# Reordering the attention steps of a hybrid backbone kernel, with earlier loads and splits

## What is computed

```python
h = modulate(rms_norm(x, g_mix[l]), mod[:, :, 0], mod[:, :, 1])
p = h @ w_in[l]                      # 6 kinds of features and 3 gates
# 4 retention heads (dk 128, dv 256), 8 latent heads (64+32 by 128),
# 8 grouped-query heads (128) over 2 key/value heads
s = jnp.einsum('bqhgd,bshd->bhgqs', q, k) * scale
pr = jax.nn.softmax(s, axis=-1)
o = jnp.einsum('bhgqs,bshe->bqhge', pr, v)
gs = jax.nn.sigmoid(gates)
z = gs[:, :, 0] * (y_ret @ w_ret_o) + gs[:, :, 1] * (y_mla @ w_mla_o) + gs[:, :, 2] * (y_gqa @ w_gqa_o)
x = x + mod[:, :, 2] * (z @ w_out)
x = x + mod[:, :, 5] * swiglu(modulate(rms_norm(x, g_ffn[l]), mod[:, :, 3], mod[:, :, 4]))
```

## Time and profile before

| | us |
|---|---|
| median of 3 runs | 3534.91 |
| lowest and highest run | 3522.54, 3536.19 |
| the profiled execution | 3530.96 |
| its span | 3528.8 |
| PE busy in it | 3240.0 |
| DVE, ACT, POOL busy | 1519.6, 1254.8, 397.4 |

### The profile page before, as it was taken

The page is one execution under the profiler, slowest core; times in us unless marked ns, Lnnn a source line. Parts: engine busy times, 40 slices in busy tenths (PEclk is TensorE's granted clock), DMA queues, the critical chain, the costliest instruction groups (busy, mean ns, idle before and its releaser), DMA issues.

```text
span 3528.8 us, 49714 instructions
## 1 busy us (share of the span) xinstructions
PE 3240.0 (92%) x18760; PEld 2735.5 (78%) x18760; DVE 1519.6 (43%) x2047; ACT 1254.8 (36%) x1777; POOL 397.4 (11%) x304
## 2 busy tenths in 40 slices
PE   6999999999898889999999978998999898889998
PEld 5788877888777777788888867877777776668886
DVE  4555424445335533422222355553455445443333
ACT  3344432454333332211211234444355433432222
POOL 0011100111101201000100101110011101011001
PEclk9999999999999999999999999999999999999999
DMA  4222141111331143123142432222221232222222
GB/s 181 78 71 73 64 136 63 60 54 59 101 121 64 42 137 126 48 96 112 64 135 70 140 111 81 75 82 84 75 71 65 75 115 68 90 100 95 95 95 101
DMA packets 100921, 315.17 MB, mean 89 GB/s; under 512 B 11088, under 2 KB 21456, under 8 KB 100816
## 3 DMA queue, kind: packets, MB, share of 16 engines
q1 hardware_dynamic: 55872, 202.40, 17.2%
q10 hardware_dynamic: 44944, 111.32, 9.4%
HBM read 283.79 MB, written 29.88 MB: 89 GB/s over the span
## 4 chain that ended last, share of the span: by engine, by line
PE 45%; issue 8%; DVE 5%; ACT 2%; POOL 1%; DMA 1%; ACTq 0%; DVEq 0%; POOLq 0%
PE ps L1417 43%; PE ps L1531 1%; POOL ptl L1399 1%; DVE mx L927 1%; ACT wh L431 1%; PE ps L1509 1%; DVE wl L896 1%; DVE ptl L945 0%; DMA mraw<-in_wmod 0%; DVE tmp L906 0%; DVE tmp L1061 0%; DVE tmp L966 0%; ACT pth L484 0%; PE ps L1441 0%; ACT side L509 0%
## 5 line engine op out<-in xcount | busy, mean ns | idle before, releaser
L1417 PE MATMUL ps<-hh,wh 128*128 128x512 f32 x2768 | 827.2, 359 | 48.5 <-DVE wl L896 25.8
L1417 PE MATMUL ps<-hl,wh 128*128 128x512 f32 x2768 | 818.8, 356 | 0.0
L1417 PE MATMUL ps<-hh,wl 128*128 128x512 f32 x2768 | 815.5, 355 | 0.0
L896 DVE TENSOR_TENSOR wl<-raw,wh 128x1024 fp32r<-128x1024 f32 x364 | 484.1, 1330 | 645.6 <-ACT wh L431 616.1
L1417 PEld LDWEIGHTS ps<-hh,wh 128*128 128x128 f32 x2768 | 454.9, 191 | 138.3 <-issue 48.6
L1417 PEld LDWEIGHTS ps<-hh,wl 128*128 128x128 f32 x2768 | 455.6, 191 | 78.3
L1417 PEld LDWEIGHTS ps<-hl,wh 128*128 128x128 f32 x2768 | 455.0, 191 | 73.8 <-issue 0.7
L431 ACT ACTIVATE wh<-raw 128x1024 fp32r<-128x1024 f32 x364 | 382.5, 1051 | 228.7 <-PE ps L1417 193.2
L1417 PE MATMUL ps<-yh,wh 128*128 128x512 f32 (+1 forms) x1296 | 412.0, 372 | 27.5 <-DVE wl L896 15.1
L1417 PE MATMUL ps<-yl,wh 128*128 128x512 f32 (+1 forms) x1296 | 398.3, 362 | 0.0
L1417 PE MATMUL ps<-yh,wl 128*128 128x512 f32 (+1 forms) x1296 | 397.4, 361 | 0.0
(11 more groups left out here) (190 smaller groups left out, 3452.5 us busy)
## 6 DMA issues: line engine op xcount, KB each, us to landing
raw<-in_stream SPq DMA_DIRECT2D x364, 512.0 KB, 3.5
mraw<-in_wmod ACTq DMA_DIRECT2D x40, 512.0 KB, 3.5
prob<-in_wmod ACTq DMA_DIRECT2D x40, 512.0 KB, 3.5
gspill<-prob ACTq DMA_DIRECT2D x32, 384.0 KB, 2.3
tmp<-gspill ACTq DMA_DIRECT2D x24, 384.0 KB, 3.1
early_y<-in_wmod SPq DMA_DIRECT2D x12, 512.0 KB, 14.6
vraw<-gspill ACTq DMA_DIRECT2D x16, 384.0 KB, 3.5
dec<-in_dec ACTq DMA_DIRECT2D x8, 768.0 KB, 4.2
```

The lines of the kernel that those rows point to most:

```text
L896: dve.tensor_tensor(wl[:, s, :], raw[:, s, :], wh[:, s, :].bitcast(F32), ALU.subtract).then_inc(sem("w_lo"), 1)
L1417: ins = pe.matmul(out, lhs[w], rhs[x](cols), start=start and n == 0, stop=stop and n == 2)
```

## The change

**Attention.** PE's step becomes: scores n, transposes of tile n-2, `fill(n)`, and on odd n a values block of tiles n-3 and n-2. ACT's and DVE's parts on the transposed tile move to the front (ACT) and ahead of `fill` (DVE). `y_hi` and `y_lo` stay behind `fill(n)` on even n. `OUTS` moves to bank 7 and `QSUM` to bank 5, so that scores 1 and 3 wait for `y_lo`, and `LAG` of y falls from 2 to 1. The queries' statistics move by `gqa_stat`: to step 3 in layer 0 and step 1 in layer 1.

```diff
-LAG = {"s_rinv": 1, "s_pn": 1, "t_ready": 2, "t_hi": 2, "t_lo": 2, "y_ready": 2, "y_hi": 2, "y_lo": 2}
+LAG = {"s_rinv": 1, "s_pn": 1, "t_ready": 2, "t_hi": 2, "t_lo": 2, "y_ready": 1, "y_hi": 1, "y_lo": 1}
...
+def gqa_stat(nq):
+
+    return nq - 3
...
-        OUTS = SCORES[0] + TOK
-        QSUM = SCORES[1] + TOK
+        OUTS = SCORES[1] + TOK
+        QSUM = SCORES[0] + TOK
...
-                        if n in (0, 2) and c.has(n - 5):
-                            pe.wait_ge(sem("y_lo"), c.v("y_lo", n // 2 - 3))
-
-                        if n == 3 and std is not None:
+                        if n in (1, 3) and c.has(n - 5):
+                            pe.wait_ge(sem("y_lo"), c.v("y_lo", (n - 5) // 2))
+
+                        if n == 2 and c.nq == 4 and std is not None:
                             pe.wait_ge(sem("v_std"), std)
...
-                    if n == 2:
-
-                        pe.wait_ge(sem("s_exp"), c.v("s_exp", 1))
-                    fill(n)
-                    if n % 2 == 0 and c.has(n - 3):
-                        values(c, n, par if n >= 3 else 1 - par)
                     m = n - 2
...
                         ins.then_inc(sem("t_ready"), 1)
+                    if n == gqa_stat(c.nq):
+                        pe.wait_ge(sem("s_exp"), c.v("s_exp", n - 1))
+                    fill(n)
+                    if n % 2 and c.has(n - 2):
+                        values(c, n, par if n >= 3 else 1 - par)
 
             def values(c, n, vpar):
-                m = n - 3
+                m = n - 2
...
-                    fill(n)
-                    if n % 2 == 0 and c.has(n - 3):
-                        y_lo(c, n // 2 - 2, home)
                     m = n - 2
...
+                    fill(n)
+                    if n % 2 == 0 and c.has(n - 3):
+                        y_lo(c, n // 2 - 2, home)
```

```diff
                     split(at, 7)
+                    split(at, 8)
...
-                    if query and n == 0:
+                    if query and n == 0 and not alone:
                         split(at, c0 + 1)
...
-                            if j == 0:
-                                split(at, 3)
+                            split(at, 2 * j + 3)
```

```diff
+            def first_load(ph):
+
+                if ph["nmod"]:
+                    mod_load(ph, 0, ph["j0"] + ph["home"] * N_MOD * KT)
...
                 elif kind == "z":
+                    first_load(ph["out"])
...
-                            mod_load(ph, 0, row0)
...
                                 if ph["nmod"] and begun:
                                     if k == 1:
-                                        mod_fold(t, r)
-                                    if k != r:
-                                        mod_row(t, k, ph)
+                                        if r:
+                                            mod_fold(t, 0)
+                                        mod_row(t, r, ph)
...
+                        if ph["nmod"] and begun:
+                            mod_fold(t, 1)
```

```diff
-                        pe.wait_ge(sem("v_lo"), t.v("v_lo"))
...
                         split(t, 2)
+                        roped(t, (0, 0), 0, 0, 1, qh, ql, 0, nt)
                         dve.wait_ge(sem("vt_hi"), t.v("vt_hi", 1))
...
-                        roped(t, (0, 0), 0, 0, 1, qh, ql, 0, nt)
```

More of the change, by code:

```diff
@@ L147, in plan @@
         raws = [SPILLED] * MLA_RAWS
-        phase("mla_first", layer, 0, {}, total(head, head, HELD, *raws, attention(nq, first=1)), nt=nt)
+        phase("mla_first", layer, 0, {}, total(
+            head, head, HELD, {"free0": -1, "free1": 1}, *raws, attention(nq, first=1)), nt=nt)
         phase("mla", layer, MLA_HEADS // 2 - 1, total(head, head, att, att, *raws, *raws), nt=nt)
@@ L192, in plan @@
     phase("final", DEPTH - 1, 0, {}, {}, nt=LAT)
-    for ph, after in zip(phases, phases[1:]):
+    for n, (ph, after) in enumerate(zip(phases, phases[1:])):
+        if ph["kind"] in ("z", "ffn"):
+            ph["out"] = next(x for x in phases[n:] if x["kind"] == "out")
         if ph["kind"].endswith("_last"):
@@ L492, in y_hi, with spill @@
                                ACT.Copy).then_inc(sem("y_hi"), 1)
-            def spill(at, kc, f, kg, nt, full, held_at, skip):
-                slot = 1 if held_at is not None and kg == 0 else 0
+            def spill(at, kc, f, kg, nt, full, slot, held_at, skip):
                 act.wait_ge(sem("product"), at.v("chunk", kc + 1))
@@ L551, in fill @@
                 def fill(n):
-                    if query and n == 0:
+                    if query and n == 0 and held_at is None:
                         split(at, c0 + 1)
@@ L991, in fill @@
                     for j, steps in enumerate(pieces):
-                        if n == steps[0]:
+                        if n == steps[0] and not (qslot and j == 0):
                             split(at, c0 + query + j + 1)
@@ L1592, in gqa_query, with raw @@
                 qs, pieces = gqa_steps(nt // P, raws, alone)
+                def raw(n):
+                    for j, steps in enumerate(pieces):
+                        if alone and n == steps[0] and j == 0:
+                            pe.wait_ge(sem("vt_lo"), at.v("vt_lo"))
+                        gate(at, c0 + query + j, j if alone else f0 + query + j, steps, n, nt, 1 - j if alone else 0)
                 def fill(n):
@@ L1602, in fill @@
                         ins.then_inc(sem("v_stat"), 1)
-                    for j, steps in enumerate(pieces):
-                        if alone and n == steps[0] and j == 0:
-                            pe.wait_ge(sem("vt_lo"), at.v("vt_lo"))
-                        gate(at, c0 + query + j, j if alone else f0 + query + j, steps, n, nt, 1 - j if alone else 0)
+                    if not alone or n != 1:
+                        raw(n)
                 return fill
```

65 lines of the change are left out of this document (35 added, 30 removed).

## The result

The changed kernel takes 3620.57 us in the median of four runs (3609.28 to 3628.53). The kernel before took 3530.35 beside it, and the ratio is 1.0255, with a 95% interval of 1.0215 to 1.0295: 2.5% slower, 90 us where 64 were forecast. It lies inside the stated range of 3530 to 3645. Single executions that took far longer than the others of their kernel (3811 and 4195 us of the kernel before, 9062 us of the one with the first heads' part alone) are left out of every ratio here. The profiled execution is 97.6 us longer than that of the kernel before (spans 3626.4 and 3528.8).

What follows compares the result with a forecast made beforehand. TensorE, busy 92% of the span, was taken as the bound. Waits +84, clock +35 and gains -55 gave +64 on the profiled run's 3530.96, so 3595, or 3599 for the median; range 3530 to 3645.

Steps and rivals of the forecast that it cites:

- Rival B: Whole kernel: the waits come but the clock stays; 3564, nearer 3555 if the chains are shorter; chance 0.25.
- C: Whole kernel: gains fail or are paid back, slow multiplication's 8 added; 3599 + 25 to 45, some 3635; chance 0.10.
- A: Whole kernel, the forecast itself: y stands behind the fill and clock falls follow; 3599; chance 0.45.
- kl waits in retention below 4: Sign in the profile after: PE's waits for kl in retention below 4; if they remain, C.
- Rival D: Scores 1 and 3: ACT and DVE reach y sooner, so PE doesn't wait; near 3468, faster; chance 0.12.
- The clock: Attention heads: long new waits make PE's clock fall, about 24 falls at 1.6 us; +35 (0 to 60).
- Retention: Retention heads: q rope before the v subtraction, 2.7 a head off layer 1's kl waits, 1.7 in layer 0; 17 (12 to 22).
- First heads: First grouped-query and latent heads: chunks split a phase ahead remove waits on wl; 10.5 and 2.5 us gained.
- the head at 2571.18: Slow grouped-query head of layer 1: loses 2.33, 0.75 and its clock fall; 5 us gained.
- The modulation rows: Merges and "out" phases: waits for modulation weight rows go; 7.5 and 12.7 us gained, 20 together.
- The two rules: Shared bank of values output and odd scores: the wait must stay; DVE multiplication slows while GpSimd works.
- the slow multiplication: DVE, ahead of the query's subtraction: 0.17 with GpSimd idle, 1.46 while it worked; 8 over six layer 1 heads.

Runs made afterwards that it cites:

- experiment 1: The changed kernel with the two y copies (ACT and DVE) moved from behind the fill to ahead of it on even steps; 3467.72 us, ratio 0.9831 to the kernel before.
- experiment 2: The kernel before with the attention part of the change alone; 3655.97 us, ratio 1.0344.
- experiment 4: The changed kernel with useless matmuls ahead of PE's wait for y in the loop heads; 3559.19 us, ratio 1.0083 to the kernel before.
- experiment 3: The kernel before with all parts of the change but the attention's (first heads, modulation rows, retention); 3498.66 us, ratio 0.9905.

## Why the prediction was right, and where it wasn't

**The mechanism.** Right. PE waits for y at scores 1 and 3, 56 times for 119.3 us, because y stands behind the fill; experiment 1 takes the loss away by moving nothing else, and experiment 2 shows that nothing else brings it. Rival B, the waits without the clock, falls by the granted clock of 0.90, 0.86 and 0.92. C's time, 3624 and more, lies nearer to the measured 3620.57 than A's 3599, but what brought the time there was the clock, and of C's conditions only one was met in part, that gains are paid back. The sign "kl waits in retention below 4" could tell nothing: the longest was 3.4 before the change. Rival D, faster because ACT and DVE reach y in time, needed the order of experiment 1: 3468 was its time, and 3467.72 the measurement. That they agree so well is luck, since D counted on 55 us of gains, and the parts alone give 33; in experiment 1's trace all outside the loops is 52 shorter, which wasn't taken apart.

**The waits.** Sized well, for the latent heads of layer 1 3.5 and 3.7 forecast against 2.92 and 3.43, for layer 0 2.8, 1.55 and 1.1 against 2.5, 1.03 and 0.86, for the grouped-query heads of layer 1 2.3 and 4.7 against 2.2 and 4.3. The sum for the 24 loop heads was 79; at full clock (experiment 4) they cost 67. By loop, with the falls that the prediction counted (at 1.6 us each) set against the changed kernel's loops less those of experiment 4:

| loop | waits, forecast | waits, measured | falls counted | clock, forecast | clock, measured |
|---|---|---|---|---|---|
| latent heads, layer 0 | 25 | 20.4 | 3 | 4.8 | 25.1 |
| grouped-query heads, layer 0 | 2 | -1.0 | 0 | 0 | -0.1 |
| latent heads, layer 1 | 31 | 27.7 | 12 | 19.2 | 33.7 |
| grouped-query heads, layer 1 | 21 | 19.9 | 9 | 14.4 | 16.7 |

**The clock.** This term failed in size: 35 forecast, and 75 measured in the traces or 61 by the medians, at or beyond the upper end of 60. The step counted one fall of 1.6 us for each wait of 3.5 and more, half a fall for each of 2.3 to 2.8, and none for shorter ones; that is 24 falls and 38 us, and 35 less those that occurred before. The price was right for a short fall and wrong for a long one. In layer 1, from scores 3 of a latent head to scores 0 of the next, the same 66 matmuls without any wait among them take, in the first and in the second head of the changed kernel:

```profile
2219.46:2234.34 14.88, 14.88 (x66) 14.59 (x67) 3.10 (x5) 2.50 (x4) 1.47 (x1) 0.50 0.11 36
2269.23:2278.81 9.58, 9.58 (x66) 9.31 (x67) 3.10 (x5) 2.50 (x4) 1.47 (x1) 0.82 0.17 55
```

and with the waits filled (experiment 4):

```profile
2197.80:2205.79 7.99, 7.99 (x66) 7.85 (x67) 3.10 (x5) 2.50 (x4) 1.47 (x1) 1.00 0.21 66
```

Both heads had waited 3.43 us. In the second the fall costs the forecast's 1.6. In the first the clock stays at half throughout, and it costs 6.9; so it is in three heads of the six, which makes 16 us more than was counted. In layer 0 it is the number of falls that was wrong. The one behind the wait of 2.5 came in all six heads and not in three, and there is another. The windows of a latent head there in the changed kernel (its value product, then its values block):

```profile
266.78:272.25 5.47, 5.47 (x36) 5.47 (x37) 2.91 (x6) 1.43 (x4) 0.61 (x1) 0.73 0.30 99
272.25:276.18 3.93, 3.93 (x20) 3.93 (x20) 0.96 (x1) 0.81 (x1) 0.00 (x0) 0.51 0.00 0
```

The same values block with y ahead of the fill (experiment 1):

```profile
255.72:257.87 2.15, 2.15 (x20) 2.15 (x20) 0.96 (x1) 0.81 (x1) 0.00 (x0) 1.00 0.05 11
```

Five of these six heads have a second fall, at their end, behind a wait of only 0.86 for the key's low part: the block takes 3.93 us in place of 2.15, and with the value product the fall costs 3.1 a head, which is the other 16 us. The wait of 0.86 is there in experiments 1 and 4 too, and the clock stays at 1.00. So the second fall comes only where the longer waits are. But they don't settle it: the sixth head has the same three waits (2.48, 1.03 and 0.87) and no second fall. Why some falls come and some last is open.

**The gains.** 55 forecast and 33 found. Retention: 17 forecast, 17 timed (11 to 23), though only in part by the way told. In layer 1 the waits for `kl` shrank by 2.0 us in all and not by 2.7 a head: 2.7 is more than the 1.76 that were moved out of the way, and two of the four had been 2.4 and 2.6 already, where 2.4 is what is left of each. The value transposes' waits, which did go, are 9.3 in both layers; the traces show 5 to 8 us in all, and where the rest of the 17 comes from was not taken apart. First heads: 13 forecast, 17 timed. The 5 for the head at 2571.18 were counted twice, for that head is one of the six whose mean of 32.28 the +3.5 a head is set against. The modulation rows failed: 20 forecast, 4 found (-1 to 8). The merges' 7.5 became nothing by themselves, because the step named no follower for the wait it took away, and the chunk's `wl` was there, as late. The "out" phases' 12.7 stand in the traces as 10 to 14, but the timed whole doesn't show them in full; what takes them back was not found.

**The sum.** 67 for the waits and 75 for the clock in the loops, less 45 for all else with the last attention phases in it, is the 97.6 between the two profiled spans. The 45 are of these two executions; by the medians the other parts take 35 off between experiment 2's kernel and the changed one, and 32 off the kernel before in experiment 3. The forecast came near with +64 for a balance in which the waits were 12 too high, the clock 26 to 40 too low and the gains some 10 to 20 too high. That the waits' error went against the other two is luck, and without it the forecast would have been further off.

**The two rules.** The wait for y stayed in every kernel, so what the Trainium skill states on a shared bank ("PSUM — Partial Sum Buffer", section "PSUM bank collisions raise a hardware error") was tried in no run. The 1.3 us of the slow multiplication didn't show in the chain to y: in the six loop heads of layer 1 it took 0.17 each time, with GpSimd idle then, and the waits were 4.26, where 4.7 was forecast without it.

## What to carry to other kernels

When a producer's output is moved next to its consumer, move its drain with it: here the output lay ready for nearly 5 us, while its two copies stood behind the copy of a product that the waiting engine itself had just made, and moving them ahead turned 2.5% slower into 1.7% faster. Price a repeated wait twice, once for its length and once for the clock, and the second may be the larger; useless matmuls in the waits measure the two apart. And for each wait that an edit removes, name the wait that is next in the same place, before booking the gain.

## What the runs showed of the hardware

A fall of the clock need not lie directly behind a long wait, and it need not be short. In a latent head of layer 0 PE stood 2.6 us until scores 1 at 282.28. The granted clock was 0.59 in the 3.7 us behind that wait, between the levels of 1.2 and 2.4 GHz, and 0.99 from 286.00 to 300.00. With waits of 1.03 and 0.86 later in such a head it was 0.73 and then 0.51, near the lower level, at the head's end (the windows above). In layer 1 it was 0.50 for 14.88 us in which PE had no wait at all, and 0.82 over the same work in the next head. The windows behind the long wait:

```profile
282.28:286.00 3.72, 3.72 (x14) 3.25 (x15) 1.88 (x5) 1.15 (x2) 0.65 (x1) 0.59 0.45 141
286.00:300.00 14.00, 14.00 (x85) 12.51 (x84) 7.95 (x11) 5.63 (x10) 2.29 (x2) 0.99 0.18 66
```

Keeping PE at useless work until y came gave the full clock back in all loops and 61 us of the time, with the scores blocks waiting for y just as long. And two executions of one kernel, the one with the modulation rows' part, differ by 5.8 us in the last 764 us. Retention's 17 us were 5 and 8 in the two traces, so a change of that size can't be measured from one trace.
